# Narrow chunks of the expert stage multiplied in pairs, with three buffers

## The reference

```python
def swiglu(h, w1, w3, w2):
    return (jax.nn.silu(h @ w1) * (h @ w3)) @ w2

def moe_swiglu(h, w_r, b_r, w1, w3, w2):
    logits = (h @ w_r).astype(jnp.float32) + b_r.astype(jnp.float32)
    top_v, top_i = lax.top_k(logits, TOP_K)
    probs = jax.nn.softmax(top_v, axis=-1)
    combine = jnp.einsum('blk,blke->ble', probs, jax.nn.one_hot(top_i, N_EXPERTS, dtype=jnp.float32))
    out = jnp.zeros_like(h)
    for e in range(N_EXPERTS):
        out = out + combine[..., e, None].astype(h.dtype) * swiglu(h, w1[e], w3[e], w2[e])
    return out
```

## Time and profile before

| | us |
|---|---|
| median of 3 runs | 1557.04 |
| lowest, highest | 1554.74, 1559.09 |
| the profiled execution | 1560.56 |
| its span, first to last instruction | 1558.8 |
| its expert stage, turns 0 to 3 | 806 to 1536 |

### The profile page before, as it was taken

One profiled execution on the slowest core, in us unless ns is written; L12 is line 12 of the kernel. 1 busy time (PEld: TensorE's weight loads), 2 busy tenths in 40 slices (PEclk: granted clock), 3 DMA queues, 4 the chain that ended last, 5 costly groups with the idle time before them and its releaser, 6 DMA issues.

```text
span 1558.8 us, 21878 instructions
## 1 busy us (share of the span) xinstructions
PE 1476.8 (95%) x8674; PEld 1041.6 (67%) x8675; DVE 838.1 (54%) x1139; ACT 619.1 (40%) x702; POOL 18.2 (1%) x60
## 2 busy tenths in 40 slices
PE   6999698999999999896989999999999999999996
PEld 4886486788888887883855576565756566555754
DVE  4799944333333333898564554445645555445552
ACT  4426723232122232549253433434443444434442
POOL 2000000000000000000000000000000000000000
PEclk8999999999999999899989999999999999999998
DMA  9734914822543234349069999989999999999992
GB/s 330 228 108 163 350 60 158 216 61 75 135 109 91 74 92 135 109 135 347 6 266 389 341 327 332 342 329 401 385 408 405 404 384 402 408 356 402 384 409 88
DMA packets 214152, 395.47 MB, mean 254 GB/s; under 512 B 12044, under 2 KB 131232, under 8 KB 214048
## 3 DMA queue, kind: packets, MB, share of 16 engines
q1 hardware_dynamic: 213456, 393.80, 70.7%
q10 hardware_dynamic: 592, 0.21, 0.1%
HBM read 392.93 MB, written 1.05 MB: 253 GB/s over the span
## 4 chain that ended last, share of the span: by engine, by line
PE 84%; DVE 6%; ACT 5%; DMA 3%; issue 2%; DVEq 0%; SPq 0%; ACTq 0%
PE bank L772 82%; DMA raw<-in_moe_w 2%; DMA raw<-in_w_mod 1%; PE bank L1301 1%; ACT w_hi L1738 1%; DVE w_lo L2370 1%; DVE tb L1913 1%; ACT la L1617 1%; DVE lr L2222 1%; DVE y L2062 0%; DVE h_lo L1921 0%; ACT lr L1611 0%; PE bank L1246 0%; ACT lm L1659 0%; DVE li L2209 0%
## 5 line engine op out<-in xcount | busy, mean ns | idle before, releaser
L2370 DVE TENSOR_TENSOR w_lo<-raw,w_hi 128x2048 fp32r<-128x2048 f32 x132 | 302.4, 2291 | 266.2 <-ACT w_hi L1738 263.3
L1738 ACT ACTIVATE w_hi<-raw 128x2048 fp32r<-128x2048 f32 x132 | 252.3, 1912 | 406.2 <-PE bank L772 275.4
L772 PE MATMUL bank<-h_hi,w_hi 128*128 128x512 f32 (+1 forms) x768 | 285.7, 372 | 14.1 <-DVE h_lo L1921 12.0
L772 PE MATMUL bank<-h_lo,w_hi 128*128 128x512 f32 (+1 forms) x768 | 282.7, 368 | 0.0
L772 PE MATMUL bank<-h_hi,w_lo 128*128 128x512 f32 (+1 forms) x768 | 282.5, 368 | 0.0
L1464 ACT ACTIVATE w_hi<-raw 128x2048 fp32r<-128x2048 f32 (+1 forms) x64 | 113.7, 1776 | 195.7 <-PE bank L772 192.8
L772 PEld LDWEIGHTS bank<-h_hi,w_hi 128*128 128x128 f32 x768 | 146.7, 191 | 41.1 <-DVE h_lo L1921 13.9
L772 PEld LDWEIGHTS bank<-h_hi,w_lo 128*128 128x128 f32 x768 | 146.7, 191 | 23.8
L772 PEld LDWEIGHTS bank<-h_lo,w_hi 128*128 128x128 f32 x768 | 147.0, 191 | 23.0
L1896 DVE TENSOR_TENSOR w_lo<-raw,w_hi 128x2048 fp32r<-128x2048 f32 (+1 forms) x64 | 135.9, 2123 | 38.6 <-ACT w_hi L1464 38.5
L772 PE MATMUL bank<-w_hi,hc_hi 128*128 128x512 f32 (+1 forms) x384 | 153.6, 400 | 2.9 <-ACT warm L1793 2.9
(11 more groups left out here) (323 smaller groups left out, 1795.7 us busy)
## 6 DMA issues: line engine op xcount, KB each, us to landing
raw<-in_moe_w SPq DMA_DIRECT2D x220, 1024.0 KB, 9.4
raw<-in_w_mod SPq DMA_DIRECT2D x48, 1024.0 KB, 8.6
raw_x<-in_moe_w SPq DMA_DIRECT2D x44, 1024.0 KB, 9.4
raw<-in_ffn_w SPq DMA_DIRECT2D x44, 512.0 KB, 5.4
raw<-in_w_in SPq DMA_DIRECT2D x18, 1024.0 KB, 5.7
raw<-in_ffn_w SPq DMA_DIRECT2D x16, 704.0 KB, 4.8
raw<-in_w_out SPq DMA_DIRECT2D x8, 1024.0 KB, 5.5
x_in<-in_ctx SPq DMA_DIRECT2D x1, 1024.0 KB, 5.0
```

The source lines that it names most:

```text
L772: return nc.tensor.matmul(dst, lhsT, rhs, start=first, stop=last)
L1738: nc.scalar.activation(w_hi[:, j % SPL, :], raw[:, E_SLOT[j], :], ACT.Copy)\
L2370: V.tensor_tensor(w_lo[:, j % SPL, :], raw[:, E_SLOT[j], :], w_hi[:, j % SPL, :].bitcast(F32), ALU.subtract).then_inc(dve_done, dve_n(name ...
```

## The change

A new function `narrow_behind` says which narrow chunks follow wide chunk j: none behind an even j, j - 1 and j behind an odd one, and 32 behind 32. PE goes by it in all turns with narrow work, for the further tokens of turn 0 too. SP's queue follows: behind an even j it issues only the wide load, behind an odd j the wide load and then the two narrow ones (in turn 0 the two narrow ones first, and then both wide ones). Since narrow chunk 0 now comes after the back step, the wait for `s_act` (the last turn's `y_s`), which it carried, is also put in front of the back step. The number of buffers, the sizes of the chunks and all arithmetic stay.

```diff
+def narrow_behind(j, two):
+
+    if not two or j % 2 == 0 and j == PER_EXPERT - 1:
+        return (j,)
+    return (j - 1, j) if j % 2 else ()
...
             def pair(e, e_s, after, after_s, n, top=False, last=False):
-                for j in range(PER_EXPERT):
+                def narrow(j):
                     if not last or j + RING < PER_EXPERT:
                         sp.wait_ge(s_pe, at("s_mm", j) + n * Ks)
                         s_chunk(e_s if j + RING < PER_EXPERT else after_s, (j + RING) % PER_EXPERT)
+
+                def wide(j):
                     t = j + RING + AHEAD
                     if not last or t < PER_EXPERT:
                         taken(j + AHEAD, n * K)
                         if top and j + AHEAD < PER_EXPERT:
                             sp.wait_ge(x_pe, at("x_mm", j + AHEAD))
                         t_chunk(e if t < PER_EXPERT else after, t % PER_EXPERT)
+
+                for j in range(PER_EXPERT):
+                    behind = narrow_behind(j, True)
+                    if not top:
+                        wide(j)
+                    for i in behind:
+                        narrow(i)
+                    for i in behind if top else ():
+                        wide(i)
...
-                    if s:
-                        s_mm(j, turn_no, first)
-                    for x in X_BEHIND[j] if top else ():
-                        x_mm(x)
+                    for i in narrow_behind(j, True) if s else ():
+                        s_mm(i, turn_no, first)
+                    for i in narrow_behind(j, True) if top else ():
+                        for x in X_BEHIND[i]:
+                            x_mm(x)
                     if j == 0 and not first:
                         if second:
                             pe.wait_ge(x_act, at("x_y"))
                         pe.wait_ge(dve_done, at("e_y", 1) - Kd + de)
+                        if s:
+                            pe.wait_ge(s_act, at("s_y") - Ksa + sa)
                         for odd in range(2):
                             back(range(odd, KD, 2), pe_done, pe_n, ("e_back", odd), x=second, s=s)
```

## The result

| | before | after |
|---|---|---|
| median, us | 1557.19 (1554.74 to 1559.09, 4 runs) | 1603.93 (1600.56 to 1608.32, 4 runs) |
| ratio of the times | 1 | 1.030, 95% interval 1.028 to 1.032 |
| profiled execution (span) | 1560.56 (1558.8) | 1600.56 (1598.8) |

The change costs 46.7 us, or 3.0%. The forecast was 24 us, with a range up to 1602 us; the direction was right, the size was not. The profiled execution of after is the fastest of its runs, so the two profiles differ by 40 us only.

The account below looks back on a forecast made before the run. PE and loads were taken as nearly equal limits (173.5 against 171.0 us in turn 2). +10.0 us in each of turns 1 to 3 and 6 less in turn 0 gave +24 on 1557.04: 1581 us, range 1560 to 1602.

Parts of the forecast that it names:

- the waits: Turns 1 to 3, each: 18 us for late narrow loads, less 4.1 (extras), plus 0.7 (column chunks) and 1 (lost cover).
- the clock: PE's clock behind new waits in turns 1 to 3: no term in the sum, lower clock only as Rival 3.
- the sum: Whole kernel: +10.0 us in each of turns 1 to 3, 6 less in turn 0, +24 on the median, 1581 us.
- turn 0: First turn: 6 us less, pairing saving 7.5 us of switches, less 1.5 for moved waits on ACT and DVE.
- The place and the length of the loop: Turns 1 to 3, from wide chunk p's end: narrow load lands at 13.3 us, PE reaches chunk p+2 at 11.05.
- the choice of 6.2 between 4.8 and 7.4: Wide load ahead of the narrow one, turns 1 to 3: 6.2 us from issue to landing, between shortest and longest read.
- the first rival: Turns 1 to 3: loads keep up, no extra beyond 2.56 us and a constant; 13.5 us less, 1543 us; chance 0.07.
- The saved switches: PE, turns 1 to 3: 16 fewer visits to narrow work a turn, 0.35 us each, 5.6 us of PE time.
- Rival 3: Turns 1 to 3: new waits also lower PE's clock, much slower, above 1600 us; chance 0.04.
- The sign for rival 3: Profile after the change: a granted PE clock under 0.97 would show that rival.

Follow-up runs that it names:

- e5: Changed kernel, but PE unpaired in turns 1 to 3 while the changed load queue order stays: 1636.2 us, ratio to before 1.049.
- e2: Changed kernel, but in turns 1 to 3 SP issues both narrow loads ahead of the odd chunk's wide load: 1566.82 us, ratio to before 1.008.
- e11: Changed kernel, but in turns 1 to 3 SP's order behind an odd chunk is narrow, wide, narrow load: 1565.72 us, ratio to before 1.007.
- e4: Kernel before (single narrow chunks) with expert loads of half the bytes, multiplying old data in place of the rest: 1552.47 us.
- e3: Changed kernel (paired) with expert loads of half the bytes, multiplying old data in place of the rest: 1541.6 us.
- e1: Changed kernel, but narrow chunks paired in turn 0 alone, turns 1 to 3 as in the kernel before: 1558.06 us, ratio to before 1.000.
- e14: Changed kernel itself, unedited, profiled another time to compare busy time and length turn by turn: 1607.42 us.
- e10: Changed kernel with only the narrow loads at half the bytes, wide loads whole, queue order as changed: 1559.3 us, ratio to before 1.001.
- e9: Changed kernel with two small unused matmuls ahead of the wait for each pair's second narrow chunk, from chunk 5 on, turns 1 to 3: 1616.12 us.
- e8: Changed kernel, but turn 0 single except chunks 6 and 7, turns 1 to 3 paired from chunk 2 on, narrow loads first: 1566.12 us, ratio to before 1.005.

## Why the prediction was wrong in size

The direction and the waits came as forecast. The step that failed is the clock: the sum had nothing for matmuls at the low clock behind the new waits, and some 10 to 12 us of it were measured. The second is turn 0, with a gain of 6 us that did not come.

- **The waits: right.** It had 15.6 us of waits a turn (18, less 4.1, plus 0.7 and 1), or 46.8 in three. The four profiles of the changed kernel have an idle PE for 52 us in turns 1 to 3, before 3.4: 48.5 more. In turns 1 to 3 of after all waits of PE for loads that pass 0.3 us stand at the second narrow chunk of a pair, and the time to landing of `raw_x` fell to 9.2 us in the median.
- **The place and the length of the loop: right in kind.** The order of the queue alone (e5, e2, e11) makes or undoes it. The terms, in the median of turns 1 to 3 of after: the wide load is issued at 4.6 us (4.5 forecast), takes 6.4 from issue to landing (6.2), and the narrow one follows 2.57 later (2.56). The sum of these is 13.6; the median landing came at 13.9 (13.3 forecast). With 13.9 the same loop asks for some 14 us more in the three turns (0.6 / 2 in each double step), and these did not come, so that the waits agree to 1.7 us is in part luck. So the choice of 6.2 between 4.8 and 7.4 held, and the first rival's load without any extra did not come: the wide loads p + 6 took 4.9 to 8.1 us. By the Trainium skill's fit ("DMA: Bandwidth & Descriptors", section "Anatomy of one DMA") a chunk is estimated at 4.4 us, less than any of them. That fit is stated for DMAs that GpSimd issues, and these are issued by SP.
- **The saved switches: right.** 5.6 us a turn forecast; in busy time of turn 2 they are 4.9 (before against e2) and 5.7 (e4 against e3).
- **The clock: the step that failed.** Rival 3 was put as another outcome, with 0.04, and not as a term of the sum. Waits of 2 us and more come some two times a turn, and behind some of the waits (1.8 to 4.3 us long) the clock is halved for some 3 us, at times for 7 or 10. Busy time of turns 1 to 3 is 523.5 us in the mean of the four profiles of the changed kernel, 511.2 in e2: 12.3 us, at about 1 us of time each. The clock's own record gives 24 us at half clock in turns 1 to 3 of the four profiles, in the mean, and 3.4 in e2: 12 us of work lost against 1.7, so some 10 of the 12.3. The other 2 stay open. I had looked at one wait of 1.6 us that left the clock alone and at one of 2.9 that did not, and then took the new waits for too short, although the sum itself put PE's wait at 2.2 us. The sign for rival 3, a clock under 0.97, was set too low as well: 0.98 over a turn of 190 us is already 4 us.
- **Turn 0: the second.** 6 us less were forecast, and e1 shows none. The switches did go: busy time fell by 6 us (197.8 in the earlier trace rows to 191.6). The waits grew by as much. The waits of turn 0 in after:

```profile
PE bank L1259 <- ACT xT L1794: 2.6, 1, 2.6
PE bank L792 <- ACT hdx L1773: 2.4, 1, 2.4
PE bank L792 <- DMA raw<-in_moe_w: 1.2, 2, 0.8
PE bank L792 <- DVE hidx L2416: 0.8, 1, 0.8
PE bank L792 <- issue: 0.7, 1, 0.7
PE bank L792 <- ACT gsx L1770: 0.7, 1, 0.7
```

  Together with two shorter ones these are 9.1 us, against 3.2 before (2.8 of them in the earlier trace rows). I had counted the waits for `gsx` that the table of chunks moves, and those went down, from 2.8 to 0.7. The two long ones are waits for the one bank that all transposes share (`TURN_BANK`, `turn_bank_free`). The first stands at chunk 8, where the selection needs the bank that ACT has yet to clear (`hdx`) of the transposes of chunk 7:

```profile
849.31 0.44 PE L1259 MATMUL bank<-ident,hidx 128*128 128x128 f32 x2
...
852.65 1.91 ACT L1761 ACTIVATE w_hi<-raw 128x2048 fp32r<-128x2048 f32 x1 [4.13 <-PE bank L792]
854.46 0.37 ACT L1773 ACTIVATE hdx<-bank 128x256 f32<-128x256 f32 x1
...
854.88 0.60 PE L792 MATMUL bank<-cw,picks 128*128 128x1 f32 x4 [2.35 <-ACT hdx L1773]
```

  ACT does that copy behind its split, as before. But before, narrow chunk 8 and a further tokens' chunk stood between wide chunk 8 and the selection, and PE did not wait:

```profile
856.00 1.94 PE L772 MATMUL bank<-raw_x,hcs 128*64 128x512 f32 x8
...
857.86 1.07 PE L772 MATMUL bank<-raw,hcx 128*32 128x256 f32 x16
858.00 0.37 ACT L1750 ACTIVATE hdx<-bank 128x256 f32<-128x256 f32 x1
...
858.86 0.61 PE L772 MATMUL bank<-cw,picks 128*128 128x1 f32 x4
```

  Now an even step holds the wide chunk alone. The other long wait is the same at chunk 22, behind the transposes of chunk 21 (`xT`). So the saved switches were given back where a short step leaves ACT no cover.

The sum again, for turns 1 to 3: switches -14.5 (e2 against before), waits +48.5, other busy time, mostly the clock, +12.3, together +46.3; turn 0 about nothing. The four profiled executions lie 45.8 above that of before in the mean, and the medians differ by 46.7. The forecast had -16.8, +46.8, 0, and -6: the two missing terms are 12.3 and 6 us, and switches and waits add 2.3 and 1.7 to the gap of 22.7.

## What to carry to other kernels

When a change lets work on one engine come in pairs, look first at the queue that feeds it: a load that is put behind another load's wait inherits that wait and that load's landing time, and here this alone cost 5% (e5). Where loads and PE lie within 2% of each other, time saved on PE turned into waiting here (e2), so ask what the loads' own floor is before counting any switch. When work moves out of a step, look at what else that step gave cover to. And price a new wait twice: its own length, and the matmuls at half clock behind it, as a term of the sum and not as a rival.

## What the hardware showed that I had not expected

- The clock's answer to a wait is not a function of its length alone: a wait of 2.04 us in turn 1 was followed by matmuls at a clock of 0.60, and one of 2.46 us at 1043.6 us, in the same turn, by a clock of 1.00. The wait of 2.6 us in turn 0 left the clock at 1.00 in one execution of the changed kernel and was followed by 0.68 in another (e14).
- A load's time to landing depends on the loads around it: the wide load took 6.4 us (median) with whole narrow loads around it and 5.2 with half ones (e10).
- The idle time behind the last turn, put down to "issue", was 3.8 to 5.3 us in most kernels and 12.0 and 12.8 in the profiles of e9 and e8, though nothing in that part of the program was changed. What it depends on stays open; it can hide or feign a difference of 0.5%.
